# The first layer's projections begun on half of the features, in a two-block transformer kernel on one core

## The reference

```python
mod = c_silu @ w_ada + b_ada
shift, scale, gate = jnp.split(mod, 3, axis=-1)
u = rms_norm(x, norm_g) * (1 + scale[:, None]) + shift[:, None]
z = u @ w_in
```

## Time and profile before

| what | us |
|---|---|
| median of 3 runs | 1461.52 (1459.36 to 1463.19) |
| the profiled execution, whole | 1457.38 |
| its span, first to last instruction | 1455.7 |

### The profile page before, as it was taken

One profiled execution on the slowest core, in us unless ns is written; L12 is line 12 of the kernel. 1 busy time (PEld: TensorE's weight loads), 2 busy tenths in 40 slices (PEclk: granted clock), 3 DMA queues, 4 the chain that ended last, 5 costly groups with the idle time before them and its releaser, 6 DMA issues.

```text
span 1455.7 us, 20251 instructions
## 1 busy us (share of the span) xinstructions
PE 1405.2 (97%) x8130; PEld 1149.9 (79%) x8130; DVE 567.0 (39%) x1335; ACT 414.6 (28%) x771; POOL 163.8 (11%) x191
## 2 busy tenths in 40 slices
PE   5999999999999999999999999999999999999996
PEld 2888788888878888888888878877777788887765
DVE  1363312201226432322244441245583533467463
ACT  1112212411021222333313222332343422433432
POOL 0110200000011021000111200013140000242000
PEclk9999999999999999999999999999999999999999
DMA  9644544355355444444333332346323433332200
GB/s 369 241 152 167 206 160 166 125 195 197 146 223 211 188 173 162 167 160 145 131 130 116 120 136 92 147 170 229 120 90 146 170 118 147 129 113 88 88 29 29
DMA packets 31486, 221.77 MB, mean 152 GB/s; under 512 B 3872, under 2 KB 4000, under 8 KB 4896
## 3 DMA queue, kind: packets, MB, share of 16 engines
q1 hardware_dynamic: 31392, 220.47, 40.7%
HBM read 219.41 MB, written 1.05 MB: 151 GB/s over the span
## 4 chain that ended last, share of the span: by engine, by line
PE 87%; DVE 7%; ACT 2%; issue 2%; DMA 1%; POOL 1%; SPq 0%; DVEq 0%; ACTq 0%; POOLq 0%
PE event L899 45%; PE event L890 9%; PE event L1043 6%; PE event L1087 5%; PE logits L975 3%; PE mixed_out L1031 3%; PE turns L994 3%; PE event L856 3%; PE event L1055 2%; PE event L1114 2%; PE event L1187 1%; DMA ring<-in_w 1%; PE event L1068 1%; PE event L878 1%; ACT S L1305 1%
## 5 line engine op out<-in xcount | busy, mean ns | idle before, releaser
L899 PE MATMUL event<-u,ring 128*128 128x256 f32 x3200 | 713.8, 381 | 4.9 <-ACT u L1223 2.5
L899 PEld LDWEIGHTS event<-u,ring 128*128 128x128 f32 x3200 | 601.7, 190 | 102.3 <-issue 20.3
L890 PE MATMUL event<-ring,u 128*128 128x256 f32 (+1 forms) x704 | 150.9, 371 | 0.0
L890 PEld LDWEIGHTS event<-ring,u 128*128 128x128 f32 x704 | 127.4, 190 | 20.9 <-issue 4.9
L2034 POOL TENSOR_TENSOR raw<-raw,tables 128x512 f32<-128x512 f32 (+1 forms) x28 | 44.6, 1592 | 736.3 <-DVE turned L1610 544.5
L1269 ACT ACTIVATE region<-event 128x512 f32<-128x512 f32 x72 | 43.0, 597 | 279.3 <-PE event L899 279.0
L1305 ACT ACTIVATE S<-logits,stat 128x512 f32<-128x512 f32 (+2 forms) x160 | 83.7, 535 | 132.6 <-DVE stat L1649 128.0
L1087 PE MATMUL event<-region,ring 128*128 128x256 f32 x384 | 85.1, 380 | 3.3 <-DVE region L1792 3.3
L1087 PEld LDWEIGHTS event<-region,ring 128*128 128x128 f32 x384 | 72.2, 190 | 15.8 <-issue 6.5
L1043 PE MATMUL event<-region,ring 128*128 128x256 f32 x384 | 84.2, 380 | 0.0
L1043 PEld LDWEIGHTS event<-region,ring 128*128 128x128 f32 x384 | 72.6, 190 | 10.7 <-issue 1.0
(11 more groups left out here) (208 smaller groups left out, 1280.3 us busy)
## 6 DMA issues: line engine op xcount, KB each, us to landing
ring<-in_w SPq DMA_DIRECT2D x204, 1024.0 KB, 4.8
tables<-in_two SPq DMA_DIRECT2D x1, 1472.0 KB, 7.8
x<-in_x SPq DMA_DIRECT2D x1, 1024.0 KB, 15.7
x<-in_ctx SPq DMA_DIRECT2D x1, 1024.0 KB, 6.5
out<-x SPq DMA_DIRECT2D x4, 256.0 KB, 2.2
tables<-in_one SPq DMA_DIRECT2D x1, 768.0 KB, 10.7
tables<-in_late SPq DMA_DIRECT2D x1, 512.0 KB, 5.6
consts<-in_common SPq DMA_DIRECT2D x1, 320.0 KB, 3.0
```

The source lines that it names most:

```text
L890: ins = mm(bank[:, t * 256:t * 256 + width], mem.u[:, q, k, t * P:(t + 1) * P], wt[:, k * 256:k * 256 + width], start=k == 0, stop=k == KB ...
L899: ins = mm(bank[:, j * 256:(j + 1) * 256], wt[:, k * 256 + j * P:k * 256 + j * P + P], mem.u[:, q, k, :], start=k == 0, stop=k == KB - 1)
```

## The change

The first layer's four leading projections (iq, ik and both halves of bq) become "lead" units of the prologue, and each is computed in two parts: blocks 0 to 3 as soon as groups 0 and 2 are there ("lead"; of the fourth only its first 128 outputs, the others as "more" behind the last transposition), blocks 4 to 7 once groups 1 and 3 are there ("rest"). Their sums stay in the four banks of `LG` and `TR` meanwhile, and ScalarE copies them from there ("take"). "lift" does for 4 blocks what "start" does for 8. The eight modulation units of the prologue ("mve") no longer go through the ring: they have places of their own in a region that is free until the gates. SyncE issues them, the first five ring units, x and the tables without a wait, x ahead of all units. The statistics come first in the prologue. In one0 the order behind the leads is: rest 0, rest 1 (both in the prologue), bv, rest 2, "dots" 0, rest 3, "dots" 1, cq, cq, ck; the second rotation of bq now stands ahead of the second picking. The seven later groups stand behind every fifth heavy item as before, counted from the fifth instead of the fourth, in a list that has lost those four projections: they begin behind the second unit of ck. The second layer is as before. In the same bytes the host lays out the eight units as an array of their own.

```diff
@@ -95,7 +95,8 @@
-UNIT_KINDS = ("mva", "proj", "merge", "out", "outa", "outb")
+LEAD = [("iq", 0), ("ik", 0), ("bq", 0), ("bq", 1)]
+UNIT_KINDS = ("mva", "lead", "proj", "merge", "out", "outa", "outb")
...
@@ -170,10 +171,11 @@
-def one_start():
-    s = [("start",)]
-    s += [proj("iq"), proj("ik"), ("rot", "iq", 0), proj("bv"), ("rot", "ik", 0), proj("bq"),
+def one_start(led):
+    s = [("take", 0), ("rot", "iq", 0), ("take", 1), ("rot", "ik", 0), proj("bv"), ("rest", 2), ("take", 2), ("rot", "bq", 0),
+         ("dots", 0), ("rest", 3), ("take", 3), ("rot", "bq", 1), ("dots", 1), proj("cq"), proj("cq", 0, 1), proj("ck")]
+    s = s if led else [("start",), proj("iq"), proj("ik"), ("rot", "iq", 0), proj("bv"), ("rot", "ik", 0), proj("bq"),
...
@@ -197,7 +199,7 @@
-    s = modulate(s, heavy(s)[3::5][:7], 2, groups)
+    s = modulate(s, heavy(s)[4::5][:7], 2, groups)
...
@@ -333,8 +335,14 @@
-PROLOGUE = [i for g in range(4) for i in group("w0", g) + [("ada", g, "w0")]]
-PROLOGUE.insert(9, ("stats",))
+def quick(g):
+    return [("mve", 2 * g), ("mve", 2 * g + 1)]
+PROLOGUE = [("stats",)] + quick(0) + [("ada", 0, "w0")] + quick(2) + [("ada", 2, "w0"), ("lift", 0), ("lead", 0), ("lead", 1)]
+PROLOGUE += quick(1) + [("lead", 2), ("ada", 1, "w0")] + quick(3) + [("lead", 3), ("ada", 3, "w0"), ("lift", 1), ("more", 3)]
+PROLOGUE += [("rest", 0), ("rest", 1)]
...
@@ -355,7 +363,7 @@
-        n["u_scaled"] = n["u_ready"] = KB * kinds.count("start")
+        n["u_scaled"] = n["u_ready"] = KB * kinds.count("start") + KB // 2 * kinds.count("lift")
...
@@ -579,6 +587,7 @@
+        self.quick = region[:, 8704:8704 + 8 * KB * 256].rearrange("p (u n) -> p u n", u=8)
...
@@ -641,6 +650,7 @@
+        self.lead = [t[:, 512 * i:512 * i + 512] for t in (self.LG, self.TR) for i in range(2)]
...
@@ -775,22 +786,40 @@
     eng.dma_start(mem.par[:, :, :], dram["par"]).then_inc(sems["params_in"], 16)
-    for u in range(RING):
-        eng.dma_start(mem.ring[:, u, :], dram["w"][u]).then_inc(sems[f"landed{u}"], 16)
+    eng.dma_start(mem.x[:, 0, :, :], dram["x"]).then_inc(sems["x0_in"], 16)
+    def quick_units(*units):
+        for i in units:
+            eng.dma_start(mem.quick[:, i, :], dram["quick"][i]).then_inc(sems[f"quick{i}"], 16)
+    def ring_units(*units):
+        for u in units:
+            eng.dma_start(mem.ring[:, u, :], dram["w"][u]).then_inc(sems[f"landed{u}"], 16)
+    quick_units(0, 1, 4, 5)
+    ring_units(0, 1, 2)
+    quick_units(2, 3)
+    ring_units(3)
+    quick_units(6, 7)
+    ring_units(4)
+    eng.dma_start(mem.tables[:, 0:1536], dram["one"]).then_inc(sems["tables_in"], 16)
     def body(w, sec):
         units = [(item, w.first[item]) for item, _, _ in w.items() if has_unit(item)]
         units.sort(key=lambda unit: sec.units().index(unit[0]))
         row = first_row(sec)
-        if sec.name == "prologue":
-            eng.dma_start(mem.x[:, 0, :, :], dram["x"]).then_inc(sems["x0_in"], 16)
         for u, (item, e) in enumerate(units):
             n = row + u + RING
             if n < ROWS:
-                last = e if item[0] == "mva" else e + sec.events(item) - 1
-                eng.wait_ge(full[last % BANKS], w.fills(last))
+                if item[0] == "lead":
+                    eng.wait_ge(sems["lead_full"], item[1] + 1)
+                else:
+                    last = e if item[0] == "mva" else e + sec.events(item) - 1
+                    eng.wait_ge(full[last % BANKS], w.fills(last))
                 slot = n % RING
...
@@ -843,11 +870,16 @@
                     eng.wait_ge(sems[f"landed{slot}"], 16 * (row // RING + 1))
-            if kind == "mva":
+            if kind in ("mva", "mve"):
                 i = item[1]
-                if i == 0 and item[2] in ("w0", "v0"):
-                    eng.wait_ge(sems["cond_ready"], w.at("cond_ready", 1))
+                if kind == "mve":
+                    wt = mem.quick[:, i, :]
+                    eng.wait_ge(sems[f"quick{i}"], 16)
+                    if i == 0:
+                        eng.wait_ge(sems["cond_ready"], w.at("cond_ready", 1))
+                elif i == 0 and item[2] == "v0":
+                    eng.wait_ge(sems["cond_ready"], w.at("cond_ready", 1 if ("cond",) in sec.script else 0))
                 if i % 2 == 0 and (sec.name != "prologue" or e >= BANKS):
...
@@ -868,9 +901,22 @@
                 ins.then_inc(full[e % BANKS], 1)
+            elif kind in ("lead", "more", "rest"):
+                n, half = item[1], int(kind == "rest")
+                wt = mem.ring[:, n, :]
+                for j in (0,) if item == ("lead", 3) else (1,) if kind == "more" else (0, 1):
+                    for k in range(KB // 2 * half, KB // 2 * half + KB // 2):
+                        if n == j == 0:
+                            eng.wait_ge(sems["u_ready"], w.at("u_ready", k + 1))
+                        ins = mm(mem.lead[n][:, j * 256:(j + 1) * 256], wt[:, k * 256 + j * P:k * 256 + j * P + P],
+                                 mem.u[:, 0, k, :], start=j == k == 0, stop=k == KB - 1, skip_group_check=True)
+                if half:
+                    ins.then_inc(sems["lead_full"], 1)
             elif kind == "stats":
-                eng.wait_ge(drained[e % BANKS], w.fills(e - BANKS))
+                if sec.name != "prologue":
+                    eng.wait_ge(drained[e % BANKS], w.fills(e - BANKS))
                 bank = mem.bank[e % BANKS]
...
@@ -1217,11 +1263,20 @@
                 eng.wait_ge(sems["rs_ready"], w.at("rs_ready", 1))
-            elif kind == "start":
-                for k in range(KB):
+            elif kind in ("start", "lift"):
+                half = KB // 2 * item[1] if kind == "lift" else 0
+                for k in range(half, half + KB // 2 if kind == "lift" else KB):
                     eng.wait_ge(sems["u_scaled"], w.at("u_scaled", k + 1))
                     act(mem.u[:, 0, k, :], mem.u[:, 0, k, :], ACT.Identity, bias=mods[:, k, 0:1]).then_inc(sems["u_ready"], 1)
                     eng.wait_ge(sems["u_ready"], w.at("u_ready", k + 1))
+            elif kind == "take":
+                n = item[1]
+                r = ropes.index(LEAD[n])
+                eng.wait_ge(sems["lead_full"], n + 1)
+                eng.wait_ge(sems["rope_done"], w.at("rope_done", r - 1))
+                act(mem.raw[:, r % 2, :], mem.lead[n], ACT.Copy, scale=HD ** -0.5 if LEAD[n][0] == "bq" else 1.0)\
+                    .then_inc(sems["lead_out"], 1)
+                eng.wait_ge(sems["lead_out"], n + 1)
             elif kind == "cond":
...
@@ -1535,24 +1590,26 @@
             eng.wait_ge(mine, w.linked())
+    def scale_gains(w, layer, a, b):
+        stt(out=mem.gs[:, a:b], in0=mem.mods[f"w{layer}"][:, KB + a:KB + b, 0], scalar=1.0,
+            in1=mem.par[:, layer, ONE_G + a:ONE_G + b], op0=ALU.add, op1=ALU.mult).then_inc(mine, 1)
+        eng.wait_ge(mine, w.linked())
     def body(w, sec):
         ropes = rope_of(sec)
         sqs = [i[1] for i in sec.script if i[0] == "sq"]
         preps = [i[1:] for i in sec.script if i[0] == "prep"]
         gap_preps = [p for p in preps if p[1] != 0]
         soft = clamped = 0
-        if sec.name in ("one0", "one1"):
-            wl = int(sec.name[-1])
-            mod = mem.mods[f"w{wl}"]
-            stt(out=mem.gs[:, :], in0=mod[:, KB:2 * KB, 0], scalar=1.0, in1=mem.par[:, wl, ONE_G:ONE_G + KB],
-                op0=ALU.add, op1=ALU.mult).then_inc(mine, 1)
-            eng.wait_ge(mine, w.linked())
+        if sec.name == "one1":
+            scale_gains(w, 1, 0, KB)
         for item, e, u in w.items():
             kind = item[0]
             one = of_one(sec, item)
             bank = mem.bank[e % BANKS]
-            if kind == "mva" and item[1] % 2 == 1:
+            if kind in ("mva", "mve") and item[1] % 2 == 1:
                 eng.wait_ge(full[e % BANKS], w.fills(e))
...
@@ -1572,9 +1629,12 @@
                 eng.wait_ge(mine, w.linked())
-            elif kind == "start":
-                eng.wait_ge(sems["rs_ready"], w.at("rs_ready", 0))
-                for k in range(KB):
+            elif kind in ("start", "lift"):
+                half = KB // 2 * item[1] if kind == "lift" else 0
+                if kind == "lift":
+                    scale_gains(w, 0, half, half + KB // 2)
+                eng.wait_ge(sems["rs_ready"], w.at("rs_ready", int(kind == "lift")))
+                for k in range(half, half + KB // 2 if kind == "lift" else KB):
                     stt(out=mem.u[:, 0, k, :], in0=mem.x[:, 0, k, :], scalar=mem.gs[:, k:k + 1],
...
@@ -1602,7 +1662,9 @@
                 eng.wait_ge(sems["rope_done"], w.at("rope_done", r - 1))
-                if name not in ("gk", "gq"):
+                if sec.name == "one0" and item[1:] in LEAD:
+                    eng.wait_ge(sems["lead_out"], LEAD.index(item[1:]) + 1)
+                elif name not in ("gk", "gq"):
                     ev = arrival(w, *(("kk", 0) if name == "nk" else item[1:]), 0)
```

19 lines of the change are left out of this document (11 added, 8 removed).

## The result

The changed kernel took 1451.05 us (median of 6 runs, 1449.52 to 1453.12), the kernel before, on the same chip, 1460.44 (6 runs, 1456.72 to 1463.19). The ratio is 0.994 with an interval of 0.9924 to 0.9956: faster, by 9.4 us between the medians. The prediction was 1452.3, with 9.2 won.

What follows compares the result with a forecast made beforehand. TensorE bounds the kernel from the first projection on, transfers and a chain of hand-overs the start before it. 9.9 − 1.86 + 1.13 = 9.2 us won, so 1452.3 us; forecast's own range 1450 to 1456, stated range 1450 to 1458.5.

Steps and rivals of the forecast that it cites:

- statistics start: Start of the kernel: x lands at 9.0 us, so after a square and its signal the statistics begin at 9.7.
- second halves: Remaining halves of the leads start at 44.4 us, 1.5 of clock loss included; the eighth unit alone would give 43.9.
- "cq": Third projection pair of the first layer starts at 64.2 us instead of 74.09, 9.9 earlier.
- pair of units at the merge: Modulation pair taken out of the start is paid behind the second branch's second merge unit: 1.86 us lost.
- wait of the first logits: Second bq rotation now precedes the second picking, so the first logits no longer wait for it: 1.13 us won.
- wait of the second logits: Picking at worst delays the first logits' masks 0.9 us with 1.2 spare, so no wait is added: 0.
- transposition ahead of the output projection: Between last merge and first output projection, its 0.53 us fits into TensorE's 1.67 wait for VectorE: no cost.
- The clock loss: TensorE nearly idle between 20 and 23.5 us, so the clock falls and the leads lose 1.5 us.
- Key picking: Picking done by 87.3 us at worst, nothing added; rival, chance 0.12: VectorE finishes late, giving 1456 to 1461 us.
- The clock did not stay at 0.50: Rival on the leads: low clock throughout from 23.5 to 44.4 us, 8.2 slower than today, 1469.7; chance 0.03.
- Transfers did not land together: Rival at the start: transfers issued at once land together, first lead at 43.0 us, result 1472; chance 0.03.
- The slow start: Rival: slower statistics, first units at 1.2 GHz and clock loss twice halve the gain, 1456 to 1458 us; chance 0.12.

Runs made afterwards that it cites:

- the filler run: Changed kernel plus products of constants, results unused, ahead of the statistics and in three gaps up to the first lead; one execution, 1450.16 us.
- the two kernels shown above: The changed kernel (1451.05 us), and the changed kernel with the first rotation of bq put behind the first picking (one execution, 1449.62 us).
- The run with whole leads: Changed kernel with the transfer order kept, but no lead product run until all eight feature blocks are there; 1462.78 us, ratio 1.0015.
- the two moves together: Kernel before with statistics and x first, plus later modulation groups moved and bq's second rotation ahead of the second picking; 1455.1 us, ratio 0.9969.
- whole leads with units first: Changed kernel with leads computed whole, all eight units transferred ahead of the weights, each lead waiting for its own weights only; 1452.52 us, ratio 0.9952.
- rotation behind the picking: Changed kernel with the second rotation of bq put back behind the second picking; 1456.41 us, ratio 0.9978.
- statistics first: Kernel before with only x transferred ahead of the units and the statistics first in the prologue, units still in the ring; 1458.4 us, ratio 0.9985.
- the last one: Changed kernel with filler products, the eighth unit ahead of the fourth lead's weights, and the second ck unit ahead of the first logits; 1448.14 us, ratio 0.9922.

## Why the prediction was right

The sum was 9.2, the medians are 9.4 apart. Its steps:

| step | predicted | measured |
|---|---|---|
| statistics start, us | 9.7 | 8.03 |
| first lead | 23.5 | 22.27 |
| second halves | 44.4 | 43.70 |
| "cq" | 64.2, 9.9 earlier | 63.55, 10.54 earlier |
| pair of units at the merge | −1.86 | −1.86 |
| wait of the first logits | +1.13 | +1.13 |
| wait of the second logits | 0 | −0.83 |
| transposition ahead of the output projection | 0 | −0.16 |

**The start** held step by step. The statistics began 1.67 earlier than worked out from the bytes. Of that, 0.41 went to the statistics (5.46 instead of 5.05) and 0.56 to the eighth unit, in at 38.40 where 38.6 was estimated; 0.70 is left at the second halves. The text had this unit bind at 43.9 if nothing else were late; it did, at 43.70, and the filler run shows that a full clock would not have bettered it. The clock loss, 1.5, was counted at the right place and size: two leads took 8.63 (7.0 + 1.6). The statistics are slow too, 5.46 where the same 16 records take 3.62 at 396.63, although the granted clock of their stretch reads 1.00 (6 to 14 us); the prediction took that slowness from a row and not from a cause, and what makes it was not shown.

**Key picking** is the term that was mis-sized. The step read: "done by 87.3 at worst", masks 0.9 late with 1.2 spare, "Nothing added". It took 9.6 for the first picking from a row without GpSimd beside it. In the changed kernel the first rotation of "bq" stands right ahead of that picking, its first two steps took 1.12 and 1.43 instead of 0.17 and 0.35, and the whole 11.3. Masks started at 87.80, 2.2 behind the end of the first logits (84.47 + 1.16), with 1.2 spare as worked out; 0.83 came through. The prediction had this disturbance as a rival, at a price of 3.7 or more; the mechanism was the one named, and the wait that it put a price on was 0.83. The Trainium skill, SBUF — State Buffer, section "SBUF: two separate sides", says that GpSimd and some of VectorE's instructions (those in a 2-port mode or with two SBUF inputs) share a pair of ports, and that whichever starts first holds it for the whole instruction. The trace agrees: in the two kernels shown above the step of 128 x 4 elements ended 0.03 after GpSimd's instruction (61.72 and 61.69; 74.87 and 74.84), and it took 0.17 where GpSimd was idle.

**The rivals.** The clock did not stay at 0.50: TensorE's stretch from 21.9 to 25.1 in the changed kernel has it, and the second halves took 7.50 for two, near the normal 7.0 and far from 14. The Trainium skill, TensorE: Matmul & The Clock Gate, section "HAM oscillation — how this bites in real kernels", has bursts of matmuls that are shorter than the DMA waits between them start slow each time. The run with whole leads agrees (0.56 over 26.80 us, with four DMA waits). The changed kernel does not test it: its only DMA wait in the leads is 0.56, and the granted clock behind it was 1.00 (36 to 40 us). Of the two falls in the kernel before that the prediction sets beside this rule, the second came behind a wait for ScalarE, 1.97 us ahead of the first projection, and not for DMA. Transfers did not land together: units 4 and 5 kept nobody waiting at 16.83, while the last unit came at 38.40. The slow start came only as a late x, in other runs (below).

**Where the agreement is luck.** By the rows the start won 8.78 and not 9.2: 0.64 more than counted ahead of "cq" and 0.99 less at the two terms that were put at nothing nearly cancel. The medians' 9.4 holds some clock besides. In 14 executions of the kernel before, taken beside the experiments, with a mean granted clock of 0.996 or 0.997, the mean time is 1458.2; the six of the changed kernel, all at 0.996 or 0.997, have 1451.2. That is 7.0, and the two profiled executions are 7.4 apart, after the 1.6 lost at 1001 us. So I put the change at 7 to 9 us, an estimate from these figures, and that forecast and medians agree to 0.2 is luck.

**What I got wrong on the way** was the reason behind it, in the expectations and not in the prediction: that computing halves while the rest arrives is what pays. Statistics first, the two moves together and units that no longer wait for the ring come to 0.9952, by the ratios 7.0 of the 8.8 us that 0.994 is, and 7.15 of 8.78 by the rows; the halves bring some 1.5 to 1.8, and with weights between the units they are what keeps TensorE busy.

## What to carry to other kernels

Where the first work of a kernel is bound by transfers, first look at which transfers wait for an engine: a ring that is refilled by a consumer passes every delay of that consumer on to the next load, and giving the first loads places of their own came with 4.6 us here, a finer order of compute with 1.6. An edit that moves work off the start is worth what it doesn't pay elsewhere: the groups took 2.4 us out of the start, and 0.3 was left. Where the intervals of a few us overlap, rows of the place that was changed tell the steps apart better than medians do, one execution though they are. Before a term is put at nothing, take its durations from rows with the same neighbour on the other engine.

## What the runs showed of the hardware

**The first transfer's arrival varies.** x landed 5.1 us after its issue in the changed kernel. With the same first four transfers the statistics began between 8.0 and 8.9 us in some kernels and between 9.4 and 10.5 in others (whole leads with units first, rotation behind the picking, statistics first, the last one); there x landed 6.6 to 7.5 after its issue. Between six runs of the changed kernel lie 3.6 us; that x makes them was not shown.

**SyncE's issue is not always cheap.** The issues of the start in the changed kernel:

```profile
2.65 1.89 SPq L794 DMA_DIRECT2D region<-in_quick  x4
...
7.48 4.16 SPq L794 DMA_DIRECT2D region<-in_quick  x2
...
12.16 6.29 SPq L807 DMA_DIRECT2D tables<-in_one  x1
```

One transfer of 1 MiB takes 0.47 to issue at first (1.89 for four). With x and ten units issued, the next two took 4.16 together, and the tables 6.29. What held them was not tried. The second of the two is the eighth unit, which TensorE waits for at 38.40, 26.8 us after its issue ended; from 6 to 40 us the transfers ran at 410 to 437 GB/s throughout, so I doubt that a quicker issue would have brought it sooner.

**The clock falls behind waits, and not always at the same ones.** It fell at 1001 us behind a wait of 2.08, and before, behind a wait of 2.10 at the same place, it did not; it fell at 91.2 us behind 3.68. Some 1.6 us went each time.

**From execution to execution, the time goes with the granted clock.** Of 67 executions of the kernel before, taken beside the experiments, the 18 with a mean granted clock of 0.997 or 0.998 took 1454.5 to 1459.4 us, and the 21 with 0.991 or 0.992 took 1460.3 to 1464.7. That is as much as the change wins.
